# Two projection chunks by quarters of K between the modulation chunks of the first phase

## The chip, the cores and the metric

The kernel runs on one core of one Trainium2 chip. The metric is the device time of one execution in microseconds (us), the median over runs. One profiled execution of the kernel before gives the trace; its page and its rows are used below. Engines: TensorE (PE for matmuls, PEld for the load of the stationary operand), VectorE (DVE), ScalarE (ACT), GpSimd (POOL), SyncE (SP), which here issues the weight DMAs.

## The reference

Two blocks in float32 on 256 tokens of width 2048. The first block has two layers, each with a modulation of its input, a wide projection, three kinds of mixing and an output projection; the second block is larger still. What the change touches is the beginning of the first layer:

```
c_act = silu(c)
mod = c_act @ w_mod[l] + b_mod[l]                  # 2048 -> 6144: shift, scale, gate
shift, scale, gate = split(mod, 3)
h = rmsnorm(x, norm_gain[l]) * (1 + scale) + shift  # 256 x 2048
proj = h @ w_in[l]                                  # 2048 -> 7504
...
bias = rel_bias[t5_bucket(pos_q - pos_k)]           # 256 x 256 x 8 heads
logits = q @ k * scale + bias                       # later, in sparse attention
```

The shift and scale of layer 0 are the modulation's columns 0 to 4095, so h needs 8 of the 12 chunks of 512 columns; the projection needs h.

## The kernel before

**Weights.** Every weight matrix is read once. SyncE brings pieces of four K tiles by 512 columns (1 MB) into the 4 slots of `raw`. For the projections each half piece is split in two: ScalarE rounds it to `w_hi` (L1158), VectorE writes the rest `w_lo` (L1719). TensorE then takes three matmuls for each K tile and each half of the tokens (L649 to L651): hi by hi, lo by hi, hi by lo, into `acc`, which has two buffers of one chunk each. A chunk of 512 columns is 16 K tiles, 2 token halves and 3 products: 96 matmuls, in 8 halves with 4 slots of `w_hi` and `w_lo`. The activations are held likewise as `ht_hi` and `ht_lo`.

**Modulation.** `c @ w_mod` is one row by a matrix. VectorE does it, `mod_piece`: for each K tile it multiplies the 512 columns by the scalar c of each partition and adds up (L1857, L1859), 16 instructions in a chunk, in two sums. `mod_sums` on TensorE then sums over the partitions with matmuls by a column of ones (L732): in the first phase 8 matmuls over both sums (`parts=2`, 16 records in the trace), later 4, after VectorE has added the two sums (`one_sum`, L1865). `mod_take` adds the bias into `modc` (L1870).

**First phase.** The first 8 modulation chunks run alone. Beside them TensorE and ScalarE look up the position bias in 24 steps: TensorE spreads bucket numbers over the partitions (`spread_keys`, L745) into `key_cols`, ScalarE makes one-hot columns of them (Abs L1291, Relu L1293), TensorE multiplies these by the table (`look_up`, L759) into `bias_cols`. `key_cols` lies in buffer 0 of `acc`, in two parts used in turn, `bias_cols` in `sps` and in buffer 1 of `acc`; ScalarE moves them out in three pieces. Three steps stand ahead of every modulation sum. The rows of x, scaled by their root mean square (L1276), are transposed (L783) and stored (L1269) in the same phase. After the eighth chunk comes `acol`, the 16 columns of scale times gain (L1949).

**First chunks.** `gemm` and `split` with `at=(0, 0)` then run positions 0 and 1, and with each of the eight halves of position 0 two tiles of h are formed from the stored rows: ScalarE writes `ht_hi` (L1195), VectorE forms the same value again (L1771) and subtracts (L1772).

**Order.** All five engines run programs written out by hand, each strictly in its order, with semaphores between them. A layer is a list of 19 positions: 14 chunks of `w_in` in the order `CHUNKS`, the tail of 336 columns (position 14) and 4 chunks of `w_out`. `PIECES` says after which half (1, 3, 5, 7) of a position a piece of the remaining 16 modulation chunks is read and worked off; the plan built from it also sets where sums are formed and taken. "Third chunk" below is position 2.

## Time and profile before

| | us |
|---|---|
| median of 3 runs (1913.2 to 1914.52) | 1913.96 |
| profiled execution | 1915.48 |
| its span | 1913.6 |

| engine | busy us | share |
|---|---|---|
| TensorE matmul | 1868.0 | 98% |
| TensorE weight load | 1560.6 | 82% |
| VectorE | 1376.0 | 72% |
| ScalarE | 981.6 | 51% |
| GpSimd | 201.3 | 11% |

The span is what the trace covers, 1.9 us less than the execution's own time. Matmuls are pipelined and their ends modelled, so a TensorE busy for 98% says that matmuls are nearly always under way, not at which rate; rates come from the distance of starts. Shares are means over phases with different limits, which is why the stretches below are looked at one by one.

### The profile page before, as it was taken

How to read it: one execution, taken by the hardware profiler on the slowest of the kernel's cores; microseconds unless marked ns; L12 is line 12 of the kernel's file. 1: busy time of each engine (PE TensorE's matmuls, PEld its weight loads, DVE VectorE, ACT ScalarE, POOL GpSimd, SP SyncE). 2: the span in 40 equal slices, each digit the busy share in tenths (PEclk: the TensorE clock that was granted, in tenths of full speed). 3: DMA queues.
4: the chain of work that ended last, by engine and by line, in shares of the span. 5: the costliest groups of instructions: out<-in, count | busy, mean ns of one | idle time of the engine just before them, and what ended most of it. 6: DMA issues, size and time to landing. Idle time of an engine off the chain costs nothing.

```text
span 1913.6 us, 24264 instructions
## 1 busy us (share of the span) xinstructions
PE 1868.0 (98%) x9056; PEld 1560.6 (82%) x9056; DVE 1376.0 (72%) x2049; ACT 981.6 (51%) x1325; POOL 201.3 (11%) x256
## 2 busy tenths in 40 slices
PE   4989999999999999999999999999999999999997
PEld 4878778888887887888888888888888888888886
DVE  8989999998896778956765544487776455665555
ACT  5454455445637444545554644476664444444464
POOL 0000002100100000210010000044432020031001
PEclk9999999999999999999999999999999999999999
DMA  9969987875885886754366565554454555557552
GB/s 349 365 233 347 347 289 239 311 267 165 288 311 178 321 315 233 236 170 157 122 220 198 176 196 188 190 174 154 162 167 154 196 180 192 180 177 255 185 184 102
DMA packets 211312, 424.28 MB, mean 222 GB/s; under 512 B 7168, under 2 KB 12044, under 8 KB 209804
## 3 DMA queue, kind: packets, MB, share of 16 engines
q1 hardware_dynamic: 209004, 413.08, 64.3%
q10 hardware_dynamic: 2208, 9.85, 1.3%
q8 instruction: 65, 1.06, 0.2%
q14 instruction: 35, 0.29, 0.0%
HBM read 418.69 MB, written 4.21 MB: 221 GB/s over the span
## 4 chain that ended last, share of the span: by engine, by line
PE 90%; DVE 5%; ACT 2%; issue 1%; DMA 1%; DVEq 0%; ACTq 0%; POOLq 0%; POOL 0%
PE acc L649 27%; PE acc L651 26%; PE acc L650 26%; DVE scr L1859 2%; PE tps L732 2%; PE sps L990 1%; DVE w_lo L1719 1%; DMA raw<-in_w_in 1%; PE tps L690 1%; PE sps L759 1%; ACT w_hi L1158 1%; PE acc L759 0%; PE tps L783 0%; DVE proj L1832 0%; PE sps L809 0%
## 5 line engine op out<-in xcount | busy, mean ns | idle before, releaser
L1719 DVE TENSOR_TENSOR w_lo<-raw,w_hi 128x1024 fp32r<-128x1024 f32 (+1 forms) x596 | 742.3, 1251 | 471.0 <-ACT w_hi L1158 468.2
L1158 ACT ACTIVATE w_hi<-raw 128x1024 fp32r<-128x1024 f32 (+1 forms) x596 | 624.4, 1051 | 800.6 <-PE acc L651 728.8
L649 PE MATMUL acc<-w_hi,ht_hi 128*128 128x512 f32 (+1 forms) x2368 | 937.3, 396 | 7.3 <-DVE ht_lo L1772 4.8
L651 PE MATMUL acc<-w_hi,ht_lo 128*128 128x512 f32 (+1 forms) x2368 | 920.5, 389 | 0.0
L650 PE MATMUL acc<-w_lo,ht_hi 128*128 128x512 f32 (+1 forms) x2368 | 918.9, 388 | 0.0
L649 PEld LDWEIGHTS acc<-w_hi,ht_hi 128*128 128x128 f32 x2368 | 445.8, 188 | 97.9 <-issue 8.1
L651 PEld LDWEIGHTS acc<-w_hi,ht_lo 128*128 128x128 f32 x2368 | 445.3, 188 | 92.9
L650 PEld LDWEIGHTS acc<-w_lo,ht_hi 128*128 128x128 f32 x2368 | 446.2, 188 | 85.7
L1859 DVE SCALAR_TENSOR_TENSOR scr<-raw,vcol,scr 128x512 f32<-128x512 f32 x266 | 189.1, 752 | 6.6
L1859 DVE SCALAR_TENSOR_TENSOR proj<-raw,vcol,proj 128x512 f32<-128x512 f32 x70 | 52.9, 796 | 2.0
L2496 POOL TENSOR_TENSOR scr<-scr 128x128 f32<-128x128 f32 x56 | 31.0, 585 | 157.6 <-DVE scr L2246 157.6
L732 PEld LDWEIGHTS tps<-kst,scr 128*128 128x128 f32 x216 | 39.7, 275 | 2.0 <-DVE scr L1859 1.1
L759 PE MATMUL sps<-proj 128*128 128x32 f32 x128 | 32.7, 386 | 8.3 <-ACT proj L1293 7.6
L759 PEld LDWEIGHTS sps<-proj 128*128 128x128 f32 x128 | 31.9, 332 | 10.4 <-ACT proj L1293 8.5
L2433 POOL COPY xn<-proj 128x128 f32<-128x128 f32 x4 | 2.5, 642 | 358.0 <-ACT proj L1350 358.0
L732 PE MATMUL tps<-kst,scr 128*128 128x1 f32 x216 | 38.9, 306 | 0.9 <-DVE scr L1859 0.7
L2467 POOL TENSOR_TENSOR proj<-proj 128x512 f32<-128x512 f32 x8 | 13.4, 1691 | 224.6 <-ACT proj L1469 193.5
L1333 ACT ACTIVATE proj<-acc,st 128x512 f32<-128x512 f32 (+1 forms) x50 | 31.4, 679 | 0.1
L2458 POOL TENSOR_TENSOR scr<-scr,proj 128x384 f32<-128x384 f32 x16 | 22.2, 1386 | 54.2 <-DVE st L2062 54.2
L2532 POOL TENSOR_TENSOR xn<-proj 128x256 f32 x16 | 19.5, 1237 | 79.3 <-DVE proj L2340 48.6
L2422 POOL TENSOR_SCALAR_AFFINE_SELECT proj<-proj 128x128 f32<-128x128 f32 (+1 forms) x8 | 6.8, 872 | 190.0 <-DVEq L2018 151.5
L1350 ACT ACTIVATE proj<-acc 128x1024 f32<-128x1024 f32 (+1 forms) x26 | 25.7, 988 | 0.0
(287 smaller groups left out, 1371.3 us busy)
## 6 DMA issues: line engine op xcount, KB each, us to landing
raw<-in_w_in SPq DMA_DIRECT2D x208, 1024.0 KB, 5.1
...
```

The lines of the kernel that those rows point to most:

```text
L649: pe.matmul(o, hi_m, w_hi[:, slot, u, 0:width], start=start, stop=False)
L650: pe.matmul(o, hi_m, w_lo[:, slot, u, 0:width], start=False, stop=False)
L651: mm = pe.matmul(o, lo_m, w_hi[:, slot, u, 0:width], start=False, stop=stop)
L732: mm = pe.matmul(tps[:, 1, j:j + 1], src[:, e, j * P:(j + 1) * P], ones, start=e == 0, stop=e == parts - 1)
L759: mm = pe.matmul(o, onehot[:, n % 2, e * w + m * P:e * w + (m + 1) * P], rb_diag, start=True, stop=True)
L1158: act.activation(w_hi[:, x % SPL, :, 0:width], raw[:, j, 2 * (x % halves):2 * (x % halves) + 2, 0:width], ACT.Copy).then_inc(hi_ready, 1)
L1333: r = act.activation(o[:, m, :], acc[:, b, m, :], func, scale=st[:, 22 + m:23 + m])
L1350: act.activation(proj[:, :, ds(base + g * step, width)], acc[:, b, :, 0:width], func)\
L1719: dve.tensor_tensor(w_lo[:, x % SPL, :, 0:width], raw[:, j, 2 * (x % halves):2 * (x % halves) + 2, 0:width], w_hi[:, x % SPL, :, 0:width]. ...
L1859: r = dve.scalar_tensor_tensor(to[:, e, :], raw[:, slot, 2 * u + e, :], v2("c", kt), to[:, e, :], ALU.mult, ALU.add)
L2458: pool.tensor_tensor(lb_s[:, b, :], bias[:, ds(h, 1), :].rearrange("p a k -> p (a k)"), mb, ALU.add).then_inc(lb_ready, 1)
L2496: pool.tensor_tensor(first_half[0], mid, first_half[1], ALU.subtract)
```

## The change

The first phase becomes four rounds. A round i works off modulation chunks i and 4 + i (four columns' worth of shift and of scale each), forms from them four columns of `acol`, the four K tiles 4i to 4i + 3 of h, and multiplies these by the same quarter of K of projection chunks 0 and 1: 48 matmuls (L809 to L811 of the new kernel), which add up in both buffers of `acc` over the four rounds. Positions 0 and 1 of layer 0 are no longer run by `gemm` and `split`.

Since `acc` is taken, `key_cols` and `bias_cols` each have one bank of `sps`. `key_cols` has one part instead of two. `bias_cols` holds four steps and is moved out six times (`bias_out`). `STEPS` gives for each round the steps ahead of the first sum, between the sums, and between the second sum and the block of matmuls. VectorE adds up both sums of each chunk itself, so each sum has 4 matmuls. ScalarE forms the tiles of h in place and rounds them in pairs (`formed_tiles`); VectorE's second forming is gone. The four modulation pieces of position 1 move to positions 9, 12, 14, 16 and 17, with one less at 11.

```diff
 FULL = (1, 3, 5, 7)
-PIECES = [{1: FULL, 2: FULL, 3: FULL, 4: FULL, 5: FULL, 6: (1, 3), 8: (1, 3, 7), 9: (1, 3, 7), 10: FULL, 11: FULL,
-           13: (3, 7), 15: (1, 3), 16: (1, 3, 7), 17: (1, 3, 7), 18: (1, 3)},
+PIECES = [{2: FULL, 3: FULL, 4: FULL, 5: FULL, 6: (1, 3), 8: (1, 3, 7), 9: FULL, 10: FULL, 11: (1, 3, 5),
+           12: (7,), 13: (3, 7), 14: (3,), 15: (1, 3), 16: FULL, 17: FULL, 18: (1, 3)},
           {1: (3, 7), 2: (1, 3, 7), 3: (1, 3, 7), 4: (1, 5), 5: (1, 5), 6: (1, 3), 8: (1, 3)}]
 RAW = 4
 SPL = 4
-TURNS = [{x: x for x in range(8)}, {p + 1: p for p in range(8)}]
+TURNS = {p + 1: p for p in range(8)}
+STEPS = [(6, 0, 2), (2, 3, 2), (2, 3, 2), (0, 2, 0)]
...
-        key_cols = acc[:, 0, :, :]
-        bias_cols = [sps[:, :, :].rearrange("p a n -> p (a n)"), acc[:, 1, :, :].rearrange("p a n -> p (a n)")]
+        key_cols, bias_cols = sps[:, 0, :], sps[:, 1, :]
...
-            with loop(sp, 8, {free: 8}) as i:
-                pieces(full(wm[0]), i * CH, CH)
             def land(slot, src, width=CH):
                 sp.wait_ge(raw_read, free.next(2))
                 sp.dma_start(raw[:, slot, :, 0:width], src).then_inc(raw_landed[slot], 16)
+            for i in range(4):
+                for n in (i, 4 + i):
+                    for q in range(4):
+                        land((10 * i + q) % RAW, full(wm[0])(q, n * CH, CH))
+                for g in range(2):
+                    land((10 * i + 8 + g) % RAW, full(wi[0])(i, CHUNKS[g] * CH, CH))
             for l in range(DEPTH):
                 for k, g in enumerate(CHUNKS + [NCH] + [0, 1, 2, 3]):
+                    if l == 0 and k < 2:
+                        continue
...
             def spread_keys(n):
-                if n >= 2:
-                    pe.wait_ge(spread_read, n - 1)
+                if n >= 1:
+                    pe.wait_ge(spread_read, n)
...
                 mm.then_inc(keys_spread, 1)
             def look_up(n):
-                if n == 16:
-                    pe.wait_ge(bias_ready, 1)
+                if n % 4 == 0 and n:
+                    pe.wait_ge(bias_ready, n // 4)
                 pe.wait_ge(onehot_ready, n + 1)
...
                 mm.then_inc(onehot_used, 1)
...
             spread_keys(0)
-            for i in range(8):
-                for n in range(3 * i, 3 * i + 3):
-                    if n < 23:
-                        spread_keys(n + 1)
-                    look_up(n)
-                pe.wait_ge(raw_read, lo.next(8))
-                mod_sums(macc[:, i % 2, :, :], parts=2)
-                if i == 2:
-                    pe.wait_ge(xs_ready, 2 * M)
-                if i >= 2 and i < 6:
-                    for k in range(4 * i - 8, 4 * i - 4, 2):
...
+            def steps(n, count):
+                for j in range(n, n + count):
+                    if j < 23:
+                        spread_keys(j + 1)
+                    look_up(j)
+            n = 0
+            for i, (a, b, c) in enumerate(STEPS):
+                steps(n, a)
+                mod_sums(macc[:, 0, :, :])
+                for k in (4 * i, 4 * i + 2):
+                    pe.wait_ge(xs_ready, M * (i + 1))
+                    if k:
+                        pe.wait_ge(xt_ready, k // 2)
...
+                    tr.then_inc(xt_turned, 1)
+                steps(n + a, b)
+                mod_sums(macc[:, 1, :, :])
+                steps(n + a + b, c)
+                n += a + b + c
+                t_lo.skip(4)
+                pe.wait_ge(turn_lo, t_lo.ahead(2))
+                lo.skip(16)
+                for g in range(2):
+                    if i == 0:
+                        pe.wait_ge(acc_taken, taken.next())
+                    for h in range(2):
+                        pe.wait_ge(raw_read, lo.next())
+                        slot = 2 * g + h
+                        for u in range(2):
+                            kt = 4 * i + 2 * h + u
                             for m in range(M):
...
+                                hi_m, lo_m = (a[:, kt, m * P:(m + 1) * P] for a in (ht_hi, ht_lo))
+                                o = acc[:, g, m, :]
+                                pe.matmul(o, hi_m, w_hi[:, slot, u, :], start=kt == 0, stop=False)
+                                pe.matmul(o, hi_m, w_lo[:, slot, u, :], start=False, stop=False)
+                                mm = pe.matmul(o, lo_m, w_hi[:, slot, u, :], start=False, stop=kt == KT - 1)
+                        mm.then_inc(split_used, 1)
+            pe.wait_ge(bias_ready, 6)
...
             for l in range(DEPTH):
-                pe.wait_ge(mod_taken, m_taken.ahead(1))
-                gemm(1, chunk_halves(2), 8, at=(l, 0), turned_x=l == 0, ready=layer_ready if l else None)
+                if l:
+                    pe.wait_ge(mod_taken, m_taken.ahead(1))
+                    gemm(1, chunk_halves(2), 8, at=(l, 0), ready=layer_ready)
...
+            def bias_out(j):
+                act.wait_ge(onehot_used, 4 * j + 4)
...
+                r.then_inc(bias_ready, 1)
+            def steps(n, count):
+                for j in range(n, n + count):
+                    o = onehot[:, j % 2, :]
+                    act.wait_ge(keys_spread, j + 1)
+                    if j >= 2:
+                        act.wait_ge(onehot_used, j - 1)
+                    act.activation(o, key_cols, ACT.Abs, bias=kst[:, C_NB:C_NB + 1]).then_inc(spread_read, 1)
+                    act.wait_ge(spread_read, j + 1)
+                    act.activation(o, o, ACT.Relu, bias=ones, scale=-1.0).then_inc(onehot_ready, 1)
+                    if j % 4 == 0 and j:
+                        bias_out(j // 4 - 1)
...
+            def scaled_rows(i):
+                if i == 0:
+                    act.wait_ge(rstd_ready, 1)
+                    act.activation(xs[:, m, i * CH:(i + 1) * CH], xres[:, m, i * CH:(i + 1) * CH], ACT.Copy,
+                                   scale=st[:, 22 + m:23 + m]).then_inc(xs_ready, 1)
+            def formed_tiles(i):
+                act.wait_ge(columns_ready, i + 1)
+                for k in range(4 * i, 4 * i + 4):
+                    scale, bias_col = of_layer(0)(k)
+                    act.activation(xt(k), xt(k), ACT.Identity, scale=scale, bias=bias_col).then_inc(tiles_formed, 1)
+                for k in (4 * i, 4 * i + 2):
+                    act.wait_ge(tiles_formed, k + 2)
+                    act.activation(ht_hi[:, k:k + 2, :], xt(k, 2).rearrange("p (e t) -> p e t", e=2), ACT.Copy)\
+                       .then_inc(turn_hi, 2)
+            n = 0
+            for i, (a, b, c) in enumerate(STEPS):
+                steps(n, a)
+                if i == 0:
                     row_root()
-                if n == 6:
-                    scaled_rows()
...
+                scaled_rows(i)
+                for k in (4 * i, 4 * i + 2):
+                    turned_rows(k)
+                steps(n + a, b)
+                for g in range(2):
...
+                        act.wait_ge(split_used, slot_free.next())
+                        act.activation(w_hi[:, 2 * g + h, :, :], raw[:, t % RAW, 2 * h:2 * h + 2, :], ACT.Copy)\
+                           .then_inc(hi_ready, 1)
+                steps(n + a + b, c)
+                n += a + b + c
+                formed_tiles(i)
+            bias_out(5)
...
-                act.wait_ge(scale_ready, l + 1)
-                split(1, 16, 8, evac=down6, at=(l, 0), flush=False, turning=TURNS[l], scales=of_layer(l),
-                      side=embedding_out if l else None)
+                if l:
+                    act.wait_ge(scale_ready, 1)
+                    split(1, 16, 8, evac=down6, at=(l, 0), flush=False, turning=TURNS, scales=of_layer(l),
+                          side=embedding_out)
+                else:
+                    act.wait_ge(split_used, SPL + 14)
+                    down6(0, 0)
...
-            def mod_turn(i, first=False):
-                for b in range(2):
+            def columns(i):
+                dve.wait_ge(mod_taken, 1 + 2 * (i + 1))
+                at = slice(4 * i, 4 * i + 4)
+                dve.scalar_tensor_tensor(acol[:, at], modc[:, KT + 4 * i:KT + 4 * i + 4], 1.0,
+                                         v1("norm_gain", 4 * i, 4), ALU.add, ALU.mult).then_inc(columns_ready, 1)
+            for i in range(4):
+                for b, cm in enumerate((i, 4 + i)):
                     for q in range(4):
-                        mod_piece(macc[:, b, :, :], q, q)
-                        if q == 1 and not (first and b == 0):
-                            mod_take(2 * i + b - 1)
+                        mod_piece(macc[:, b, :, :], q, (10 * i + q) % RAW, one_sum=True)
+                        if b and q == 1:
+                            mod_take(i)
+                            if i == 0:
+                                row_inverse()
...
+                for g in range(2):
+                    t = (10 * i + 8 + g) % RAW
+                    m_land[t].skip(16)
+                    for h in range(2):
+                        dve.wait_ge(hi_ready, hi.next())
+                        dve.tensor_tensor(w_lo[:, 2 * g + h, :, :], raw[:, t, 2 * h:2 * h + 2, :],
+                                          w_hi[:, 2 * g + h, :, :].bitcast(F32), ALU.subtract).then_inc(raw_read, 1)
+                        own.skip(1)
+                    if g == 0:
+                        mod_take(4 + i)
+                        columns(i)
+                for k in (4 * i, 4 * i + 2):
+                    dve.wait_ge(turn_hi, t_hi.next(2))
+                    t_lo.skip(2)
+                    dve.tensor_tensor(ht_lo[:, k:k + 2, :], xt(k, 2).rearrange("p (e t) -> p e t", e=2),
+                                      ht_hi[:, k:k + 2, :].bitcast(F32), ALU.subtract).then_inc(turn_lo, 2)
```

TensorE, first phase, kernel before: the third and fourth of eight groups, each three lookup steps and a sum, with transposes (L732 sum, L783 transposes, L745 spread, L759 lookup).

```order
L732 MATMUL tps<-kst,scr 128x1 x8
L783 MATMUL tps<-kst,proj 128x128 x8
L745 MATMUL acc<-proj 128x256 x2
L759 MATMUL sps<-proj 128x32
L759 MATMUL acc<-proj 128x32
L759 MATMUL sps<-proj 128x32
L759 MATMUL acc<-proj 128x32
```

TensorE, kernel after, round 1, behind the 48 matmuls of round 0 (L738 sum, L789 transposes, L751 spread, L763 lookup, L809 first of the block).

```order
L811 MATMUL acc<-w_hi,ht_lo 128x512
L751 MATMUL sps<-proj 128x256 x2
L763 MATMUL sps<-proj 128x32 x4
L751 MATMUL sps<-proj 128x256 x2
L763 MATMUL sps<-proj 128x32 x4
L738 MATMUL tps<-kst,scr 128x1 x4
L789 MATMUL tps<-kst,proj 128x128 x8
L751 MATMUL sps<-proj 128x256 x2
L763 MATMUL sps<-proj 128x32 x4
```

The first sum of a round now stands behind a block and two steps, the second behind transposes and three more steps.

ScalarE, kernel before, a group of the first phase: moves of transposed rows, then steps.

```order
L1269 ACTIVATE proj<-tps 128x512 x2
L1291 ACTIVATE proj<-acc,kst 128x512
L1293 ACTIVATE proj<-proj,kst 128x512
L1291 ACTIVATE proj<-acc,kst 128x512
L1293 ACTIVATE proj<-proj,kst 128x512
```

ScalarE, kernel after, the second half of round 1: the last of three steps (L1306, L1308), a move of bias columns (L1295), the splits (L1351), two steps, the forming of h (L1330) and its rounding (L1333).

```order
L1306 ACTIVATE proj<-sps,kst 128x512
L1308 ACTIVATE proj<-proj,kst 128x512
L1295 ACTIVATE scr<-sps 128x8x32 x2
L1351 ACTIVATE w_hi<-raw 128x1024 x4
L1306 ACTIVATE proj<-sps,kst 128x512
L1308 ACTIVATE proj<-proj,kst 128x512
L1306 ACTIVATE proj<-sps,kst 128x512
L1308 ACTIVATE proj<-proj,kst 128x512
L1330 ACTIVATE proj<-proj,modc,acol 128x256 x4
L1333 ACTIVATE ht_hi<-proj 128x512 x2
```

The splits stand behind the steps between the sums, the forming of h behind two more. VectorE, kernel after, one round:

```order
L1901 TENSOR_SCALAR scr<-raw,vcol 128x512 x2
L1903 SCALAR_TENSOR_TENSOR scr<-raw,vcol,scr 128x512 x14
L1909 TENSOR_TENSOR scr<-scr 128x512
L1901 TENSOR_SCALAR scr<-raw,vcol 128x512 x2
L1903 SCALAR_TENSOR_TENSOR scr<-raw,vcol,scr 128x512 x6
L1914 TENSOR_TENSOR modc<-tps,vcol 128x4
L1903 SCALAR_TENSOR_TENSOR scr<-raw,vcol,scr 128x512 x8
L1909 TENSOR_TENSOR scr<-scr 128x512
L1991 TENSOR_TENSOR w_lo<-raw,w_hi 128x1024 x2
L1914 TENSOR_TENSOR modc<-tps,vcol 128x4
L1973 SCALAR_TENSOR_TENSOR acol<-modc,vcol 128x4
L1991 TENSOR_TENSOR w_lo<-raw,w_hi 128x1024 x2
```

Before, the same engine had only L1857, L1859 and L1870 in this phase. L1914 waits for TensorE's sums, L1991 for ScalarE's `w_hi`, and the two `ht_lo` instructions behind the last row for ScalarE's `ht_hi`.

## Rows read from the trace of the kernel before

**Rows 1.** Busy time, instructions, granted clock, DMA share and GB/s by stretch.

```profile
core 0: us, PE busy (x) PEld busy (x) DVE busy (x) ACT busy (x) POOL busy (x), PEclk, DMA share, GB/s
40.00:51.00 11.00, 9.23 (x44) 8.63 (x45) 10.79 (x20) 9.08 (x12) 0.00 (x0) 1.00 1.05 381
95.00:110.00 15.00, 15.00 (x83) 14.99 (x81) 13.48 (x22) 7.53 (x11) 0.00 (x0) 1.00 0.95 327
119.00:125.40 6.40, 6.12 (x15) 4.82 (x16) 6.26 (x12) 4.36 (x7) 0.00 (x0) 1.00 0.51 164
```

**Rows 2.** Timeline of VectorE: start, us, engine, line, operation, tiles; modulation chunks.

```profile
17.59 0.88 DVE L1857 TENSOR_SCALAR scr<-raw,vcol 128x512 f32<-128x512 f32 x2
...
40.03 0.86 DVE L1857 TENSOR_SCALAR scr<-raw,vcol 128x512 f32<-128x512 f32 x2
...
45.16 0.16 DVE L1870 TENSOR_TENSOR modc<-tps,vcol 128x4 f32 x1
...
50.96 0.88 DVE L1857 TENSOR_SCALAR scr<-raw,vcol 128x512 f32<-128x512 f32 x2
```

**Rows 3.** Timeline of TensorE: projection matmuls, first three chunks, and modulation sums.

```profile
119.28 0.77 PE L649 MATMUL acc<-w_hi,ht_hi 128*128 128x512 f32 x1 [4.81 <-DVE ht_lo L1772]
...
120.27 0.63 PE L651 MATMUL acc<-w_hi,ht_lo 128*128 128x512 f32 x1
120.70 0.63 PE L649 MATMUL acc<-w_hi,ht_hi 128*128 128x512 f32 x1
...
126.11 0.39 PE L651 MATMUL acc<-w_hi,ht_lo 128*128 128x512 f32 x1
126.33 0.39 PE L649 MATMUL acc<-w_hi,ht_hi 128*128 128x512 f32 x1
...
165.80 0.95 PE L732 MATMUL tps<-kst,scr 128*128 128x1 f32 x8
166.60 0.49 PE L649 MATMUL acc<-w_hi,ht_hi 128*128 128x512 f32 x1
...
188.51 0.95 PE L732 MATMUL tps<-kst,scr 128*128 128x1 f32 x8
189.32 0.49 PE L649 MATMUL acc<-w_hi,ht_hi 128*128 128x512 f32 x1
```

**Rows 4.** Timeline of TensorE: lookup, modulation sums, transposes.

```profile
24.20 0.64 PE L759 MATMUL sps<-proj 128*128 128x32 f32 x2 [5.91 <-ACT proj L1293]
...
29.88 3.55 PE L732 MATMUL tps<-kst,scr 128*128 128x1 f32 x16
...
35.24 0.61 PE L745 MATMUL acc<-proj 128*128 128x256 bf16 x2
...
37.21 0.61 PE L745 MATMUL acc<-proj 128*128 128x256 bf16 x2
...
80.75 1.12 PE L783 MATMUL tps<-kst,proj 128*128 128x128 f32 x4 [0.69 <-ACT proj L1269]
...
85.06 1.91 PE L759 MATMUL sps<-proj 128*128 128x32 f32 x8 [0.69 <-ACT scr L1296]
```

**Rows 5.** Timeline of VectorE around the start of the third chunk.

```profile
160.45 0.69 DVE L1865 TENSOR_TENSOR scr<-scr 128x512 f32<-128x512 f32 x1
...
164.86 2.36 DVE L1719 TENSOR_TENSOR w_lo<-raw,w_hi 128x1024 fp32r<-128x1024 f32 x2
```

**Rows 6.** Groups of ScalarE, 17 to 118 us: line, shapes, count | busy, mean ns.

```profile
L1293 ACT ACTIVATE proj<-proj,kst 128x512 f32<-128x512 f32 x24 | 17.3, 722 | 0.8
L1291 ACT ACTIVATE proj<-acc,kst 128x512 f32<-128x512 f32 x24 | 16.4, 682 | 14.3 <-PE acc L745 14.3
...
L1158 ACT ACTIVATE w_hi<-raw 128x1024 fp32r<-128x1024 f32 x2 | 2.1, 1048 | 3.1 <-DVE acol L1949 3.1
L1195 ACT ACTIVATE ht_hi<-proj,modc,acol 128x256 fp32r<-128x256 f32 x3 | 1.7, 585 | 0.0
```

**Rows 7.** VectorE's waits for splits at positions 9, 14, 17: us, times, longest.

```profile
DVE w_lo L1719 <- ACT w_hi L1158: 2.9, 2, 2.4
...
DVE w_lo L1719 <- ACT w_hi L1158: 5.2, 4, 2.1
...
DVE w_lo L1719 <- ACT w_hi L1158: 1.1, 1, 1.1
```

166 lines of the change are left out of this document (62 added, 104 removed).

## The prediction, made before the changed kernel was run

> **What bounds the kernel now.** I read the stretch table by engine first, then the timeline of VectorE and TensorE up to 220 us, then who waited for whom. The stretch table [rows 1] is to show that the first phase is a different kernel from the rest: from 40 to 51 us VectorE works 10.79 of 11.00 us while 16 DMA engines move 381 GB/s, and TensorE is issuing but slowly. The timeline of VectorE [rows 2] gives the beat of that phase: one modulation chunk begins at 17.59, and one takes from 40.03 to 50.96, 10.93 us, of which the adding into modc is 0.12. From 95 to 110 us TensorE has no free moment [rows 1], and VectorE waits for its sums. The first projection matmul starts at 119.28 and that of the third chunk (position 2) at 166.60 [rows 3]; between them lie 192 matmuls. Behind 166.60 the next chunk follows at 189.32, 22.7 us later [rows 3]: 96 matmuls at 0.2275 us are 21.8 us and a modulation sum the remaining 0.8 (188.51 to 189.32 [rows 3]), so TensorE has no gap there; it is the bound and stays it. What counts is therefore one number: when TensorE can begin the third chunk. Before, that is 166.60.
>
> **TensorE's rate.** In the first block the matmuls of 512 columns start 0.43 us apart (120.27, 120.70), from 125.4 on 0.2275 apart (126.11, 126.33) [rows 3]. That is 1.2 and 2.4 GHz, although the granted clock reads 1.00 all along [rows 1]. The small work of the first phase also runs at the lower level: 16 records of a modulation sum take 3.55 us, the 8 records of one at 165.80, behind dense matmuls, 0.80 to the next start [rows 3, 4]. So a step of the bias lookup (two spreads, four lookups), 1.97 us from 35.24 to 37.21 [rows 4], fills TensorE and does not bring the clock up, from 24 to 114 us.
>
> **The change, part by part.** Removed: the two chunks from 119.28 to 166.60, with the 4.8 us in which TensorE stood before them [rows 3], and four modulation pieces in the second. Added: four rounds, each with two modulation chunks, one block of 48 matmuls (a quarter of K for two chunks), its splits and its four columns of h.
>
> VectorE's work in a round: two chunks of 10.8 us, each with one more addition of 0.65 (the row at 160.45 is 0.69 from start to end) [rows 5], four splits of 1.14 (two in 2.36 at 164.86) [rows 5], two writes of ht_lo of 0.62 and small ones, 0.45: 22.9 + 4.6 + 1.25 + 0.45 = 29.2 us. Four rounds from 17.6 us on would end at 134.5. DMA needs less: ten pieces a round at 2.74 us (four in 10.95) are 27.4. ScalarE needs 14 steps' instructions of 0.68 and 0.72, four splits of 1.05 and four columns of 0.59 [rows 6], some 20 us. TensorE at the lower level: 7 steps 13.8, two sums of half the former matmuls 3.6, transposes 1.1 + 0.7 + 1.1 (the row at 80.75) [rows 4], and the block. I take the block as 14 matmuls at 0.427 and 34 at 0.2275, as in the first block before: 13.7 us. Together 34 us, more than VectorE's 29.2.
>
> None of the engines can run by itself, since each round is a circle: block, steps, first sum, steps, second sum, columns, block. I set the three queues side by side in their new order with these durations. A middle round, from the end of one ht_lo to the next, at TensorE's lower level:
> - VectorE: first chunk 11.45 and half of the second 5.13, then it wants the first sum. TensorE has 13.7 of the block, 3.9 of two steps and 1.8 of the sum, 19.5 in all: wait 3.0.
> - The rest of the chunk, 0.12 + 6.33. Then the splits want w_hi. ScalarE has it behind the transposes (2.9), 1.4 until the first step is going, three steps and one move of bias columns: wait 4.0. (The move itself holds TensorE 0.65, as at 85.06, 0.69 [rows 4], five times.)
> - Splits, the second sum, the columns: 4.9. Then ht_lo wants ht_hi. ScalarE has four w_hi, two steps (2.7) and the forming (2.0 and 1.1): wait 3.75. Then 1.25.
> The sum is 40.0 us, 10.8 of it waits. Round 0 starts at 17.6 and has its ht_lo at 54.4: six steps lie ahead of its first sum, 24.2 (its first lookup [rows 4]) + 6 x 1.97 + 0.65 = 36.7 and the sum to 38, where VectorE wanted it at 34.2. Rounds 1 and 2 take 40.2 and 40.6. Round 3 has no steps ahead and 30.6. That makes 165.8, and with the last block 179.5 us.
>
> If the clock stays at 2.4 GHz after the first block, steps take ScalarE's 1.4 us instead of 1.97, sums 0.8 and blocks 10.9: rounds of 36.2, 34.0 and 30.2, end 165.7. Rows show only that the small work does not raise the clock, not how fast it falls again. I take a value inside, 172.0, close to the middle, because the blocks are the smaller part of a round and the rows before 110 us are of the same kind as what lies between them. Bounds: 158.0, if even round 0 ran at the rate of the row at 165.80; 206.6, if no block got above 1.2 GHz (48 x 0.427 = 20.5 each).
>
> The Trainium skill (TensorE: Matmul & The Clock Gate, "HAM oscillation — how this bites in real kernels") says that bursts of matmuls with waits between fall back to half rate in each wait and begin slow again. By that rule every block has its slow beginning; if in addition only full standstill counted as a wait, steps would stay fast and the third chunk would begin near 170, else at up to 179.5. The trace has no second burst to test it on.
>
> Angles and lower bound (3.8 us of VectorE between the addition that ends at 161.1 and the split at 164.86, which came just in time for the third chunk [rows 3, 5]) now lie under the last block: VectorE is through 4 us after its ht_lo, and split 0 of the third chunk waits for ScalarE's move of the first chunk out of acc, which wants the block's first 24 matmuls; the other 24 (5.5 us) cover the move, w_hi and the split (1.0 + 1.05 + 1.2). So it costs nothing; without that cover it would be 3.3. VectorE's head start of some 3 us in the third chunk is worth nothing, since TensorE had no gap there.
>
> The sum at 165.80 (modulation chunk 8's) now comes after the third chunk, not before it: +0.8. The four modulation pieces taken out of the second chunk go to others, 2.9 us of VectorE each. At position 14 (the tail) VectorE waited 5.2 us, at position 9 2.9 [rows 7]: hidden. At position 17 it waited only 1.1 [rows 7], so up to 1.8 of the piece shows on VectorE, while TensorE is up to four half-chunks behind. I take +0.5 for all, bounds 0 and +4.
>
> Sum: 172.0 - 166.6 = +5.4; +0.8; +0.5: +6.7 on the profiled execution's 1915.48 (its span and 1.9 around it), 1922.2. The median of the runs lies 1.5 under it: 1920.7. I say 1920.5.
>
> **The rivals.**
> (a) The clock stays up after the first block, 165.7: -0.9 + 1.3, on the median 1914.4. For it: no stretch without TensorE work in a round need be long. Against it: more than 40% of the time between blocks is the work that left the clock low before 119 us.
> (b) Faster: the waits in the circle are mostly hidden and VectorE's 29.2 us a round decide, or the clock is up from round 0. Then 158.0: -8.6 + 1.3, 1906.7; with no waits whatever, 134.5 + 13.7 = 148 and 1897. For it: TensorE's and ScalarE's sums of work allow it. Against it: the order forces three waits of 3 to 4 us in a middle round.
> (c) No block gets above 1.2 GHz: 206.6, +41, 1955. Against it: in the first block the clock rose after 6.1 us of dense matmuls, and each block is 10.9 or longer.
> (d) As forecast, but the moved pieces come through at positions 16 and 17, where eight pieces in 21.8 us are as much as the DMA engines moved at their best: +3.5, 1924.0.
> (e) The lookup in smaller parts breaks up steps more than 0.65 five times, or the change does nothing at its place: within the range.
>
> **The numbers.** Forecast 45%, (a) 24%, (b) 19%, (c) 4%, (d) 8%. What a measurement of this kernel can tell from no change is 0.2%, 3.8 us, so faster is below 1910.2 and slower above 1917.8. Faster is (b) and the lower end of (a), whose spread is 3: 0.22. Slower is (c), (d) and five sixths of the forecast, whose spread is 4: 0.50. The rest, 0.28, is within. The likeliest case alone spans 1916 to 1925. To leave out no more than two in ten the range goes down into (b), 1905, and up past (d), 1929.
>
> **What would show it.** In the new profile: TensorE's first matmul of the third chunk at 172 (165.7 for a, under 160 for b). VectorE waiting for tps sums at the first sum of rounds 0 to 2, 3 to 4 us each, for w_hi before the first split in rounds 1 and 2, for ht_hi before every ht_lo. Blocks 40 us apart rather than 30 to 34. Start distances of 0.43 in the first third of each block; steps 1.97 apart right behind a block speak for the forecast, 1.4 for (a). From the third to the last chunk the two kernels should run at one distance to within 2 us. The forecast is wrong if blocks are 33 us apart or less, or if the distance changes after the third chunk.

## The result and the profile after

The changed kernel takes 1921.18 us (1920.62 to 1922.66, 6 runs) against 1913.69 (1913.16 to 1915.24, 6 runs) of the kernel before: a ratio of 1.0039, 95% interval 1.0026 to 1.0052. It is 7.5 us slower; 1920.5 was forecast. Its profiled execution took 1922.2 us, with a span of 1920.3.

What the forecast hung on, the third chunk's first matmul on TensorE's timeline (start, us, engine, line, operation), corresponds to 166.60 in [rows 3]; the row above it is the last matmul of the fourth block:

```profile
172.28 0.39 PE L811 MATMUL acc<-w_hi,ht_lo 128*128 128x512 f32 x1
172.50 0.39 PE L655 MATMUL acc<-w_hi,ht_hi 128*128 128x512 f32 x1
```

The forecast was 172.0. VectorE's timeline shows how the rounds got there; a round ends where its `ht_lo` (L2000) is written. These are all its waits over 0.4 us from 17 to 158 us, rounds 0 to 3 in turn:

```profile
38.54 0.16 DVE L1914 TENSOR_TENSOR modc<-tps,vcol 128x4 f32<-128x4 f32 x1 [3.54 <-PE tps L738]
52.89 1.29 DVE L2000 TENSOR_TENSOR ht_lo<-proj,ht_hi 128x512 fp32r<-128x512 f32 x2 [2.86 <-ACT ht_hi L1333]
...
81.29 2.36 DVE L1991 TENSOR_TENSOR w_lo<-raw,w_hi 128x1024 fp32r<-128x1024 f32 x2 [3.26 <-ACT w_hi L1351]
...
89.39 1.29 DVE L2000 TENSOR_TENSOR ht_lo<-proj,ht_hi 128x512 fp32r<-128x512 f32 x2 [2.79 <-ACT ht_hi L1333]
...
108.90 0.16 DVE L1914 TENSOR_TENSOR modc<-tps,vcol 128x4 f32<-128x4 f32 x1 [1.13 <-PE tps L738]
...
118.01 2.36 DVE L1991 TENSOR_TENSOR w_lo<-raw,w_hi 128x1024 fp32r<-128x1024 f32 x2 [2.48 <-ACT w_hi L1351]
...
120.98 0.16 DVE L1914 TENSOR_TENSOR modc<-tps,vcol 128x4 f32<-128x4 f32 x1 [0.61 <-PE tps L738]
...
126.92 1.29 DVE L2000 TENSOR_TENSOR ht_lo<-proj,ht_hi 128x512 fp32r<-128x512 f32 x2 [3.30 <-ACT ht_hi L1333]
...
157.24 1.29 DVE L2000 TENSOR_TENSOR ht_lo<-proj,ht_hi 128x512 fp32r<-128x512 f32 x2 [0.46 <-ACT ht_hi L1333]
```

Rounds end at 54.1, 90.6, 128.1 and 158.4: 36.5, 37.5 and 30.3 us apart. TensorE is late once for long, with the first sum of round 0; in the two middle rounds the long waits are for ScalarE, with `w_hi` and with `ht_hi`; in round 3 nobody is late. The stretch table of the three rounds, from one `ht_lo` to the next (columns as in [rows 1]), says the same in sums:

```profile
54.10:90.60 36.50, 31.32 (x142) 25.93 (x142) 29.10 (x44) 19.82 (x33) 0.00 (x0) 0.75 0.84 290
90.60:128.10 37.50, 31.71 (x156) 27.39 (x156) 29.08 (x44) 19.96 (x32) 0.00 (x0) 0.68 0.84 284
128.10:158.40 30.30, 21.07 (x92) 17.51 (x92) 28.90 (x44) 11.37 (x18) 0.00 (x0) 0.73 0.90 311
```

VectorE works 29.1 us in each (29.2 was worked out). The granted clock, 1.00 throughout in [rows 1], now reads 0.68 to 0.75. TensorE's timeline of round 2 (its 48 dense matmuls are "the block") shows what the clock does around a block:

```profile
90.75 0.80 PE L809 MATMUL acc<-w_hi,ht_hi 128*128 128x512 f32 x1 [1.38 <-DVE ht_lo L2000]
91.34 0.63 PE L810 MATMUL acc<-w_lo,ht_hi 128*128 128x512 f32 x1
91.76 0.63 PE L811 MATMUL acc<-w_hi,ht_lo 128*128 128x512 f32 x1
...
96.46 0.43 PE L810 MATMUL acc<-w_lo,ht_hi 128*128 128x512 f32 x1
96.72 0.40 PE L811 MATMUL acc<-w_hi,ht_lo 128*128 128x512 f32 x1
...
104.44 0.40 PE L751 MATMUL sps<-proj 128*128 128x128 bf16 x4
104.67 1.03 PE L763 MATMUL sps<-proj 128*128 128x32 f32 x8
...
107.83 1.03 PE L738 MATMUL tps<-kst,scr 128*128 128x1 f32 x8
108.72 0.63 PE L789 MATMUL tps<-kst,proj 128*128 128x128 f32 x4
110.13 1.06 PE L789 MATMUL tps<-kst,proj 128*128 128x128 f32 x4 [0.78 <-ACT proj L1315]
...
113.22 1.92 PE L763 MATMUL sps<-proj 128*128 128x32 f32 x8
```

The block begins at 1.2 GHz (starts 0.43 apart) and reaches 2.4 GHz at 96.5 (starts 0.23 apart). The steps, the sum and the first transposes behind it still run at 2.4 GHz, a lookup in 1.03 us; from the transposes at 110.13 on the same work takes 1.06 instead of 0.63 and a lookup 1.92. So behind the last dense matmul (104.21) the clock is still up at 108.72 and down at 110.13, with TensorE at small work between but for two waits of 0.90 and 0.78. In the four blocks 11, 13, 13 and 14 of the 47 distances between starts are slow ones (over 0.35 us).

Behind the third chunk the distance between the two kernels was to stay within 2 us. I matched L655 of after with L649 of before by number:

| place | before | after | distance |
|---|---|---|---|
| position 2 (third chunk) | 166.60 | 172.50 | 5.90 |
| position 4 | 212.76 | 218.55 | 5.79 |
| position 5 | 242.42 | 246.44 | 4.02 |
| position 14 (tail) | 477.20 | 481.26 | 4.06 |
| position 15 | 495.93 | 502.27 | 6.34 |
| position 15, second half | 507.51 | 513.54 | 6.03 |
| position 17, beginning | 541.69 | 548.52 | 6.83 |
| in layer 1 | 639.17 | 645.90 | 6.73 |

It falls by 1.8 at position 4, rises by 2.3 at position 14, falls by 0.3 in position 15 and rises by 0.8 at the beginning of 17 (the extra sum, 547.71). From 639 on it stands at 6.73 up to the last chunk (6.74 at 1892.23), and the spans differ by 6.7. The rise at 14 shows on VectorE, first before, then after (start, us, engine, line):

```profile
481.19 1.40 DVE L1719 TENSOR_TENSOR w_lo<-raw,w_hi 128x672 fp32r<-128x672 f32 x1 [2.13 <-ACT w_hi L1158]
...
485.39 0.76 DVE L1807 TENSOR_TENSOR ht_lo<-tps,ht_hi 128x256 fp32r<-128x256 f32 x2 [0.76 <-ACT ht_hi L1224]
```

```profile
483.22 4.95 DVE L1903 SCALAR_TENSOR_TENSOR scr<-raw,vcol,scr 128x512 f32<-128x512 f32 x4
488.21 0.69 DVE L1909 TENSOR_TENSOR scr<-scr 128x512 f32<-128x512 f32 x1
...
491.89 0.76 DVE L1851 TENSOR_TENSOR ht_lo<-tps,ht_hi 128x256 fp32r<-128x256 f32 x2 [0.17 <-ACT ht_hi L1242]
```

and on TensorE, which had no wait there before:

```profile
492.70 0.66 PE L696 MATMUL tps<-kst,proj 128*128 128x128 f32 x4 [1.67 <-DVE ht_lo L1851]
```

The piece and its closing addition hold VectorE for 5.7 us (483.22 to 488.90), where a piece alone takes 2.9; `ht_lo`, before at 485.39, comes 6.5 later, where the kernels stand 4.1 apart. Of that, 2.1 us are in two instructions of the piece, which took 1.81 and 1.77 us instead of 0.74 while GpSimd worked beside them:

```profile
484.64 2.98 POOL L2534 TENSOR_TENSOR proj<-proj 128x512 f32<-128x512 f32 x2 [96.17 <-ACT proj L1525]
```

```profile
483.89 0.74 DVE L1903 SCALAR_TENSOR_TENSOR scr<-raw,vcol,scr 128x512 f32<-128x512 f32 x1
...
484.67 1.81 DVE L1903 SCALAR_TENSOR_TENSOR scr<-raw,vcol,scr 128x512 f32<-128x512 f32 x1
...
486.40 1.77 DVE L1903 SCALAR_TENSOR_TENSOR scr<-raw,vcol,scr 128x512 f32<-128x512 f32 x1
```

Before, GpSimd's same two instructions (480.58 to 483.7) met VectorE mostly waiting, and one split, which took 1.40 instead of 0.86 (the row at 481.19).

### The profile page after: what moved, and what is told of

Same layout as the page of the kernel before. It is cut to its first block, busy times and chain, and to the rows that moved or that the text cites. A ratio compares the mean times of both kernels' runs of the same rounds, so it can differ in the third digit from the quotient of the medians.

```text
span 1920.3 us, 23983 instructions
## 1 busy us (share of the span) xinstructions
PE 1856.1 (97%) x8992; PEld 1542.1 (80%) x8992; DVE 1376.3 (72%) x2036; ACT 984.1 (51%) x1344; POOL 201.4 (10%) x256
## 4 chain that ended last, share of the span: by engine, by line
PE 91%; DVE 4%; ACT 3%; issue 1%; DMA 0%; ACTq 0%; DVEq 0%; POOLq 0%; POOL 0%
PE acc L655 27%; PE acc L657 26%; PE acc L656 26%; DVE scr L1903 1%; PE sps L1018 1%; PE tps L696 1%; PE sps L763 1%; PE tps L738 1%; PE acc L809 1%; PE acc L810 1%; PE acc L811 1%; ACT w_hi L1351 1%; ACT w_hi L1186 1%; DVE w_lo L1779 0%; DVE proj L1876 0%
## 5 line engine op out<-in xcount | busy, mean ns | idle before, releaser
L1779 DVE TENSOR_TENSOR w_lo<-raw,w_hi 128x1024 fp32r<-128x1024 f32 (+1 forms) x580 | 720.5, 1249 | 465.6 <-ACT w_hi L1186 463.3
L1186 ACT ACTIVATE w_hi<-raw 128x1024 fp32r<-128x1024 f32 (+1 forms) x580 | 606.5, 1051 | 773.4 <-PE acc L657 687.1
L655 PE MATMUL acc<-w_hi,ht_hi 128*128 128x512 f32 (+1 forms) x2304 | 910.4, 395 | 2.4 <-DVE ht_lo L1839 1.9
L657 PE MATMUL acc<-w_hi,ht_lo 128*128 128x512 f32 (+1 forms) x2304 | 894.0, 388 | 0.0
L656 PE MATMUL acc<-w_lo,ht_hi 128*128 128x512 f32 (+1 forms) x2304 | 892.1, 387 | 0.0
L655 PEld LDWEIGHTS acc<-w_hi,ht_hi 128*128 128x128 f32 x2304 | 432.8, 188 | 90.0 <-issue 3.2
L2563 POOL TENSOR_TENSOR scr<-scr 128x128 f32<-128x128 f32 x56 | 31.0, 585 | 157.6 <-DVE scr L2313 157.6
L763 PEld LDWEIGHTS sps<-proj 128*128 128x128 f32 x192 | 39.2, 302 | 8.4 <-ACT proj L1308 4.4
L763 PE MATMUL sps<-proj 128*128 128x32 f32 x192 | 40.4, 370 | 3.8 <-ACT scr L1295 1.5
L809 PE MATMUL acc<-w_hi,ht_hi 128*128 128x512 f32 x64 | 30.1, 471 | 9.0 <-DVE ht_lo L2000 9.0
L2534 POOL TENSOR_TENSOR proj<-proj 128x512 f32<-128x512 f32 x8 | 13.2, 1668 | 226.3 <-ACT proj L1525 192.7
L1306 ACT ACTIVATE proj<-sps,kst 128x512 f32<-128x512 f32 x24 | 16.3, 680 | 30.7 <-PE sps L751 30.7
L751 PE MATMUL sps<-proj 128*128 128x256 bf16 (+1 forms) x64 | 13.6, 335 | 17.3 <-ACT proj L1306 11.7
L810 PE MATMUL acc<-w_lo,ht_hi 128*128 128x512 f32 x64 | 29.0, 453 | 0.0
```

Of the source, the lines that this page charges most:

```text
L655: pe.matmul(o, hi_m, w_hi[:, slot, u, 0:width], start=start, stop=False)
L656: pe.matmul(o, hi_m, w_lo[:, slot, u, 0:width], start=False, stop=False)
L657: mm = pe.matmul(o, lo_m, w_hi[:, slot, u, 0:width], start=False, stop=stop)
L763: mm = pe.matmul(bias_cols[:, c:c + KPG * NH], onehot[:, n % 2, e * w + m * P:e * w + (m + 1) * P], rb_diag, start=True, stop=True)
L809: pe.matmul(o, hi_m, w_hi[:, slot, u, :], start=kt == 0, stop=False)
L810: pe.matmul(o, hi_m, w_lo[:, slot, u, :], start=False, stop=False)
```

## Experiments

All are edits of the changed kernel, timed beside the kernel before. A round is again counted from one `ht_lo` to the next.

**The piece of position 14.**

```diff
-           12: (7,), 13: (3, 7), 14: (3,), 15: (1, 3), ...
+           12: (5, 7), 13: (3, 7), 15: (1, 3), ...
-                        if k == 14:
-                            SUM_AT[n], TAKE_AT[n] = (l, k + 1, 7), (l, k + 2, 3)
+                        if k == 13:
+                            SUM_AT[n], TAKE_AT[n] = (l, k + 2, 7), (l, k + 3, 3)
```

> The changed kernel, but the modulation piece of position 14 (the chunk behind the tail) is put at position 12, and its sum and take keep their place around position 15/16. Theory: the piece and the closing addition (4.95 + 0.69 us on VectorE at 483.2 to 488.8) make ht_lo late for TensorE's turned pairs and are the +2.3 us that the distance to the kernel before gains between the first and second half of position 14. Then the distance stays at 4.1 behind position 14, TensorE's waits for ht_lo L1851 (1.7 us) are gone, and the time is about 1918.9. Rival: the wait moves with the piece (VectorE is late at position 12 or 13 instead) or was not its doing: 1921.2, no change.

1918.62 us (11 runs), ratio to before 1.0025 (1.0016 to 1.0034). The distance to before is 2.30 at position 5, 2.30 in the second half of position 14 and 2.29 at 15: the rise is gone, no other has come, and among TensorE's waits from 172 to 900 us only those that the kernel before has too are left:

```profile
PE acc L655 <- DVE ht_lo L1839: 1.9, 3, 0.9
PE acc L655 <- issue: 0.4, 1, 0.4
```

The theory holds: the distance is the same ahead of the tail and behind it, and the time came 0.3 under the 1918.9 worked out. This execution also began its third chunk at 170.71 instead of 172.50 with the same code up to there: its first two blocks had 6 and 11 slow distances where the other had 11 and 13, and its rounds 1 and 2 took 35.7 and 37.1 us. So two executions of the same code put the third chunk 1.8 us apart, and such a difference between two single profiles can be chance; the medians of several runs are the ones to compare. That the earlier rise of the clock made the difference fits these rows and is not shown by itself.

**The steps out of the rounds.**

```diff
-STEPS = [(6, 0, 2), (2, 3, 2), (2, 3, 2), (0, 2, 0)]
+STEPS = [(6, 0, 2), (0, 0, 0), (0, 0, 0), (0, 0, 0)]
 ...                      # behind the last block, TensorE and ScalarE:
+            steps(n, 24 - n)
```

> The changed kernel, but the 16 lookup steps of rounds 1 to 3 are moved behind the last block; nothing is left out. It is made to read the rounds, not to be quick. Theory (the circle of queues: steps that stand ahead of w_hi and of the forming on ScalarE make VectorE wait 3.3 and 2.8 us a round): rounds 1 and 2 fall from 36.5 and 37.5 us to VectorE's 29.2 plus about 1, as round 3 now has (30.3); the fourth block starts near 145 instead of 158.6. Rival (TensorE's slow clock or the DMA queue sets the round, not the steps' place): rounds 1 and 2 stay above 33. The 16 steps then take 16 x 1.4 to 16 x 1.97 = 22 to 32 us behind the block: third chunk at 181 to 191 and the time 1930 to 1940.

The stretches of its three rounds:

```profile
53.90:84.20 30.30, 17.83 (x72) 14.65 (x72) 28.90 (x45) 9.53 (x15) 0.00 (x0) 0.83 0.92 317
84.20:114.90 30.70, 16.43 (x72) 13.59 (x72) 28.93 (x45) 9.92 (x15) 0.00 (x0) 0.72 1.00 346
114.90:145.20 30.30, 16.43 (x72) 13.61 (x72) 28.90 (x45) 9.12 (x15) 0.00 (x0) 0.73 0.99 342
```

Rounds of 30.3, 30.7 and 30.3 with the clock nearly as low as before (0.72 to 0.83): the middle rounds' 36.5 and 37.5 come from the steps standing in them, and the rest is VectorE. The low clock by itself costs these rounds nothing; it can count only through the steps. The size behind was missed (one execution): the third chunk began at 194.78 and the time was 1947.34. The 16 steps took 33 us (158.0 to 190.8), all but the first three at the low rate, and then came ScalarE's `w_hi` behind them (TensorE waited 4.0) and a chunk that began slow.

**TensorE kept busier.**

```diff
                 b_t = bucket_b[:, 0:S] if n < 16 else bucket_b[:, S:S + P]
+                for _ in range(3 if 8 <= n < 24 else 0):
+                    pe.matmul(key_cols[:, 0:S + P], key_pick[:, 0:P], bucket_b[:, 0:S + P], ...)
 ...
+                if i:
+                    pe.wait_ge(xt_ready, 2 * i + 2)
+                    for _ in range(6):
+                        pe.matmul(tps[:, 0, 0:S + P], key_pick[:, 0:P], bucket_b[:, 0:S + P], ...)
                 t_lo.skip(4)
                 pe.wait_ge(turn_lo, t_lo.ahead(2))
```

> The changed kernel with TensorE kept busier: three more matmuls of 384 columns (bf16, their result is overwritten) ahead of each spread of steps 8 to 22, six more ahead of the blocks of rounds 1 to 3. Theory one (the fallen clock is what the rounds cost over 34): the blocks of rounds 1 to 3 start at 0.2275 us a matmul instead of 0.427 for the first 12 to 15, a block is 11 us instead of 13.7, steps are 1.5 to 1.7 apart instead of 1.97, the third chunk starts at 166 to 168 instead of 172.5, time about 1916. Theory two (the fillers do not hold the clock, or the round hangs on VectorE and ScalarE anyway): blocks still begin at 0.427 and every filler costs its time at the low rate, up to 1 us a step; third chunk at 174 to 180, time 1923 to 1929.

> The changed kernel with six more matmuls (384 columns, bf16, into the bank of the finished transposes) ahead of the blocks of rounds 1 to 3 alone; the fillers within the steps, which cost 0.93 us each at the low clock in the run before, are gone. Theory (what comes right ahead of the block decides its beginning): as with the fillers of both kinds, only 2 or 3 matmuls of a block start 0.43 apart instead of 12 to 15, a block is about 11.5 us instead of 13.7; less some 0.5 us by which the fillers overhang VectorE's ht_lo. Third chunk at 167 to 169 instead of 172.5, time 1916 to 1918. Rival (it was the busier steps that held the clock): 12 or more slow starts as before, third chunk at 173 to 174.5, time 1922 to 1923.

With both kinds of filler 1926.75 us, ratio 1.0067 (1.0051 to 1.0082), third chunk at 175.1: theory two. The fillers in the steps do not bring the clock up; the block behind the six, in round 2, has only two slow distances, as its timeline shows:

```profile
89.11 1.15 PE L750 MATMUL sps<-proj 128*128 128x384 bf16 x3
90.05 0.63 PE L753 MATMUL sps<-proj 128*128 128x256 bf16 x2
90.48 1.75 PE L765 MATMUL sps<-proj 128*128 128x32 f32 x8
92.05 2.11 PE L800 MATMUL tps<-proj 128*128 128x384 bf16 x6
93.70 0.88 PE L815 MATMUL acc<-w_hi,ht_hi 128*128 128x512 f32 x1
94.38 0.63 PE L816 MATMUL acc<-w_lo,ht_hi 128*128 128x512 f32 x1
94.81 0.43 PE L817 MATMUL acc<-w_hi,ht_lo 128*128 128x512 f32 x1
95.08 0.40 PE L815 MATMUL acc<-w_hi,ht_hi 128*128 128x512 f32 x1
```

Three fillers take 0.94 us of a step (89.11 to 90.05) and the lookup behind them still 1.75. With the six alone, 1920.47 us (5 runs, 1.0034, 1.0021 to 1.0048), which the intervals do not tell from the changed kernel, and the third chunk at 170.9, between the two that were expected. My 2 to 3 slow distances were read off one block of the other run, whose later ones had 8 and 10. With the six alone blocks 1 to 3 have 7, 9 and 10 instead of 13, 13 and 14, and are 0.9 to 1.1 us shorter; but the same blocks have 11, 8 and 9 in the run below in which TensorE sums the halves, and 7, 7 and 8 in the one with the steps behind, both without a filler. So that six fillers shorten a block is not shown. They run at the low rate themselves, 1.65 us (89.03 to 90.68), nearly all of it in a stretch in which TensorE had waited 1.38: the block began 0.14 us behind the end of `ht_lo` instead of 0.06.

**The first sum taken late.**

```diff
-                        if b and q == 1:
-                            mod_take(i)
-                            if i == 0:
-                                row_inverse()
+                        if b and q == 1 and i == 0:
+                            row_inverse()
+                        if b and q == 3:
+                            mod_take(i)
```

> The changed kernel, but VectorE takes the first sum of a round behind the second chunk's last piece instead of behind its second; the row inverse stays where it is. Theory (a take behind the last piece is hidden, the sum being long there): the waits of 3.54 us at 38.5 (round 0) and 1.1 us at 108.9 (round 2) go; in round 0 the second sum comes some 2 to 3 us earlier, ht_lo ends at 51 to 52 instead of 54.1; in round 2 the later wait for w_hi takes up what is won. Third chunk at about 170, time 1918.5. Rival: ScalarE, not the take, sets round 0 (its two steps and the forming stand behind transposes): ht_lo waits 2.9 + 3.5 there, third chunk at 172.5 and the time 1921.

1919.03 us (8 runs), ratio 1.0025 (1.0014 to 1.0035), third chunk at 169.1. The waits at 38.5 and 108.9 are gone and round 0 ends 2.05 us earlier, at 52.1, held by ScalarE from there:

```profile
50.80 1.29 DVE L2000 TENSOR_TENSOR ht_lo<-proj,ht_hi 128x512 fp32r<-128x512 f32 x2 [3.21 <-ACT ht_hi L1333]
```

The middle rounds are 35.8 and 37.2 us; in the second the wait for `w_hi` grew from 2.48 to 3.18, as expected.

**TensorE sums the halves again.**

```diff
-                        mod_piece(macc[:, b, :, :], q, (10 * i + q) % RAW, one_sum=True)
+                        mod_piece(macc[:, b, :, :], q, (10 * i + q) % RAW)
-                mod_sums(macc[:, 0, :, :])
+                pe.wait_ge(raw_read, 20 * i + 16)
+                mod_sums(macc[:, 0, :, :], parts=2)     # the second sum likewise, 20 * i + 24
```

> The changed kernel with one of its parts undone: in the rounds the two halves of a modulation chunk are summed by TensorE again (8 matmuls instead of 4 for a sum), the closing addition on VectorE (0.65 us, eight times) is gone. Theory (rounds 1 and 2 hang on ScalarE's steps ahead of w_hi, round 0 on the first sum): what VectorE wins it waits, and a sum is 1.8 us longer at the low clock where TensorE's queue counts; round 3, which is VectorE's, wins at most 1.3. Third chunk at 171 to 176, time 1920 to 1924. Rival (VectorE sets every round): 8 x 0.65 = 5.2 us less, 1916.

1926.7 us (4 runs), ratio 1.0069 (1.0054 to 1.0085), third chunk at 176.56. The rival is out, and the theory erred in size: the longer sum adds to the path twice in a round. VectorE now waits for sums 5.97 us in round 0, and 2.31 and 2.03 in round 1 where it had waited 0 and 0.33, besides 4.00 for `w_hi`. The closing addition on VectorE is the one part of the change whose undoing I tried, and it pays, by some 5.5 us.

**The steps inside the blocks.** ScalarE is idle for 12.7 to 13.7 us in each block; a step there finds its one-hot columns ready.

```diff
-STEPS = [(6, 0, 2), (2, 3, 2), (2, 3, 2), (0, 2, 0)]
+STEPS = [(6, 0, 2, 6), (0, 0, 0, 6), (0, 0, 0, 4), (0, 0, 0, 0)]
 ...                      # TensorE, behind each six matmuls of a block
+                            if 2 * slot + u >= 7 - d and 2 * slot + u < 7:
+                                steps(n, 1)
+                                n += 1
 ...                      # ScalarE, behind formed_tiles(i)
+                steps(n, d)
+                n += d
```

> The changed kernel, but the 16 lookup steps behind round 0 stand inside the blocks (6, 6 and 4 of them, one behind each six matmuls), where ScalarE was idle for 12 us; round 0 is left as it is. Theory (the place of the steps makes the round): VectorE no longer waits for w_hi, and 0.5 to 1 us for ht_hi; rounds 1 to 3 are 30.3 to 32 us instead of 36.5, 37.5, 30.3; a block grows by 6 x 1.2 = 7 us and hides. Last ht_lo ends at 146 to 149 instead of 158.4, third chunk at 160 to 163, time 1909 to 1912. Rival (TensorE takes VectorE's place: steps inside a block wait for ScalarE or bring the clock down, 2 us or more each): blocks of 26 us and more, rounds 33 to 35, time 1914 to 1918.

1917.59 us (11 runs), ratio 1.0017 (1.0008 to 1.0026), third chunk at 167.94. The time is the rival's, the mechanism is not. Steps in a block neither wait nor bring the clock down, 1.2 us each, but the first block is 20.4 us long (54.1 to 74.5), and the first sum stands behind it, while VectorE still wants that sum in the middle of the second chunk:

```profile
75.51 0.16 DVE L1920 TENSOR_TENSOR modc<-tps,vcol 128x4 f32<-128x4 f32 x1 [4.38 <-PE tps L738]
87.42 1.29 DVE L2006 TENSOR_TENSOR ht_lo<-proj,ht_hi 128x512 fp32r<-128x512 f32 x2 [0.46 <-ACT ht_hi L1337]
```

Rounds of 34.7, 35.1 and 31.6; VectorE waits 4.38, 4.48 and 1.31 for the first sum in them, and without these waits they would be 30.3 to 30.7. The late take, worth 2 us alone, had to come with it.

**All of it together.** Late take, piece at 12, steps in the blocks, and another round 0:

```diff
+STEPS = [(3, 4, 1, 6), (0, 0, 0, 6), (0, 0, 0, 4), (0, 0, 0, 0)]
```

> As the one with the steps in the blocks, and in round 0 three steps ahead of the first sum, four ahead of the second and one behind (instead of 6, 0, 2), the first sum taken behind the second chunk's last piece, and the piece of position 14 at 12. Theory (these three stand at other places and add up): round 0's ht_lo ends at 49 to 51 instead of 54.1, the third chunk starts at 155.5 to 159, 2.3 us go behind it; time 1902 to 1906. Rival (they overlap: ScalarE's four steps ahead of the second sum come in the way of w_hi, round 0 ends at 53 or later): 1907 to 1910.

1910.45 us (11 runs), ratio 0.9981 (0.9972 to 0.9990): faster than the kernel before. The rounds came (31.7, 32.0, 30.4), round 0 did not: it ended at 56.8, as the rival had it, and the third chunk began at 163.8 instead of 155.5 to 159. Four steps ahead of the splits on ScalarE made VectorE wait:

```profile
48.87 2.36 DVE L1997 TENSOR_TENSOR w_lo<-raw,w_hi 128x1024 fp32r<-128x1024 f32 x2 [7.22 <-ACT w_hi L1355]
```

Its timeline shows a step in a block at the high clock, 1.18 us on top of six matmuls (from 62.23 to 77.49 stand six steps and 36 matmuls of 0.2275):

```profile
64.95 0.39 PE L751 MATMUL sps<-proj 128*128 128x256 bf16 x2
65.18 0.98 PE L763 MATMUL sps<-proj 128*128 128x32 f32 x8
...
67.47 0.39 PE L751 MATMUL sps<-proj 128*128 128x256 bf16 x2
67.70 0.98 PE L763 MATMUL sps<-proj 128*128 128x32 f32 x8
```

Three variants of round 0 followed, all with late take and the piece at 12. The first two also put the transposes ahead of the first sum and the row inverse behind the second chunk's first piece.

```diff
+STEPS = [(4, 0, 0, 7), (0, 0, 0, 7), (0, 0, 0, 6), (0, 0, 0, 0)]   # four ahead
+STEPS = [(5, 0, 0, 7), (0, 0, 0, 6), (0, 0, 0, 6), (0, 0, 0, 0)]   # five ahead
+STEPS = [(6, 0, 2, 6), (0, 0, 0, 6), (0, 0, 0, 4), (0, 0, 0, 0)]   # six ahead, as changed
```

> Steps in the blocks, late take and piece of 14 at 12 as in the run before, but round 0 has four steps ahead of its first sum and none behind (7, 7 and 6 in the blocks), its row inverse stands behind the second chunk's first piece, and the transposes go ahead of the first sum. In the run before, ScalarE's queue gave VectorE w_hi 7.2 us late in round 0 (four steps stood ahead of it) and ht_lo ended at 56.8 instead of 49 to 51. Theory (what stands ahead of w_hi on ScalarE sets the round): round 0 ends at 48.5 to 50, rounds 1 and 2 are 32 with blocks of 22 us, round 3 31; third chunk at 156 to 158, time 1902 to 1905. Rival (round 0 is held by TensorE's lookups at the low clock and the row inverse, rounds by the longer blocks): round 0 ends at 52 or later or rounds of 33 and more, third chunk at 160 or later, 1907 and more.

> As the one with four steps ahead, with five there and 7, 6 and 6 in the blocks. Theory: round 0 1.2 to 2 us later (50 to 51.5), rounds 1 and 2 each up to 1 us shorter; third chunk at 157 to 158.5, time 1903 to 1905. Rival: the rounds don't depend on a step more or less in a block, and it is 1 to 2 us slower than with four.

> The same, but round 0 in the changed kernel's order (6 steps, 0, 2), the row inverse in its old place, 6, 6 and 4 steps in the blocks. It separates round 0 from the blocks. Theory: round 0 ends at 52.1 as with the late take alone, rounds are 31.7, 32.0 and 30.3 as in the run before; third chunk at 159, time 1905.5. Rival: round 0's order was not what held the run before (56.8): it ends again at 55 or later, time 1909 to 1911.

| kernel | rounds end | us (median, 5 runs) | ratio to before, 95% interval |
|---|---|---|---|
| four ahead | 48.1, 81.5, 117.4, 147.7 | 1903.57 | 0.9943 (0.9929 to 0.9956) |
| five ahead | 50.6, 86.0, 117.1, 147.5 | 1903.27 | 0.9943 (0.9929 to 0.9956) |
| six ahead | 52.0, 83.0, 114.5, 144.9 | 1905.76 | 0.9956 (0.9942 to 0.9969) |

All three times came as expected, and so did the ends of round 0 (48.1 is 0.4 earlier). The rounds and the third chunk of the first two did not come in their profiled executions (161.0 and 160.8 instead of 158.5 at the latest); the third has its chunk at 157.6, 1.4 early. The stretch of round 1 of the last one, with six steps in the block, shows that little is left to win, VectorE working 28.97 of 30.9 us:

```profile
52.10:83.00 30.90, 23.11 (x132) 18.95 (x132) 28.97 (x45) 18.61 (x31) 0.00 (x0) 0.90 0.90 306
```

The profiled executions of the first two took 1908.4 and 1908.2 us, the slowest of their five, so their rounds are not those of the median. In them one round of each is 35.4 or 35.9 us, where a block with seven steps had 15 slow distances, with slow steps between them, and lasted 25 us, and the sum came 4.2 to 4.3 us late. The other block with seven steps made a round of 33.4. Seven steps in a block are at the limit; with six and the late take VectorE waited for no sum longer than 0.4 us. The first two are 10.8 and 11.1 us faster than the kernel before; their intervals don't tell them apart from each other.

## Why the forecast was right, point by point

**When the third chunk starts.** Forecast 172.0, measured 172.50, and 1.8 earlier in another execution. That the circle of queues, and not VectorE's 29.2 us alone, decides the middle rounds was right, and the direction of the whole followed from it. The size is in part luck: no term gave 172.0, it was set by judgement between 165.7 and 179.5. That the fourth block covers the third chunk's first split came true: the chunk begins 0.22 us behind the block's last matmul, with no wait.

**Round 0.** 54.4 was worked out, 54.1 measured, the wait for the first sum 3.54, where the steps ahead of it end at 38.

**The block.** 13.7 us were taken for each, by the beginning of the first block before. They take 13.2 to 13.9. The Trainium skill (TensorE: Matmul & The Clock Gate, "HAM oscillation — how this bites in real kernels") says that matmuls in bursts with waits between start each burst slow. The trace agrees, with 11 to 14 slow distances in each of the four, although between these blocks TensorE did small work for most of the time and did not only wait.

**The middle rounds.** Here each of my two cases held for a part of the round. I had worked out 40.2 and 40.6 for TensorE low between blocks and 36.2 and 34.0 for TensorE high, and took a value inside by judgement. It was high for the first steps, the sum and the transposes behind each block and low from there, so the measured 36.5 and 37.5 lie between. The first step right behind the block of round 1 took 1.17 us (67.48 to 68.65), by my own sign one for case (a). The step that failed is the wait of 3.0 us for the first sum: behind a block two steps and the sum take 3.7 us (67.48 to 71.2), not 5.7, and VectorE waits 0 and 1.1. The waits for `w_hi` (4.0 forecast, 3.26 and 2.48) and `ht_hi` (3.75; 2.79 and 3.30) are there. Together VectorE waits 6.4 and 7.5 us in the two rounds, where 10.8 were worked out. With the steps taken out the first two vanish and the third is 0.46 to 0.82: the circle of queues is shown, not argued. I had written 40 us between blocks, and that 33 or less would refute the forecast; they are 36.5, 37.5 and 30.3 apart, the last with 30.6 worked out.

**Rival (a), the clock staying up, and (b), waits hidden.** (a) is the case of 36.2, 34.0 and 30.2; it fell because the clock does fall, in the middle of the small work, and fillers did not hold it to the next block. (b) is what the experiments made true by another order: with six steps in a block and a late take the rounds are 30.4 to 32.0. The bound of 148 for no waits whatever stays out of reach by some 10 us in the version whose rounds are shortest (third chunk at 157.57). Rival (c) is out, each block rises.

**Behind the third chunk.** I took +0.8 for the sum and +0.5 for the moved pieces. The sum came, +0.8. Of the pieces I had looked at position 17 and called 14 hidden, because VectorE waited 5.2 us there [rows 7]. That is the step that failed: +2.3 at 14. A piece is 2.9 us by itself, but stretched beside GpSimd's work and with its closing addition it was 5.7, and it stood directly ahead of an `ht_lo` that TensorE needed. The sum of waits over a position said nothing of that place. It was made up by -1.8 at position 4, which I did not foresee. TensorE's weight loads waited 1.5 us there before for VectorE's query products and 0.4 after; why VectorE was ahead was not tried. Rival (d) named the mechanism but the wrong positions, 16 and 17. The forecast's last condition, a constant distance to within 2 us, was therefore broken (5.9, 4.0, 6.8), and the total of +0.8 behind the third chunk instead of +1.3 is right by cancellation. So is the profiled 1922.2, hit to a tenth: the third chunk came 0.5 later than forecast and the rest cost 0.5 less.
